# A new order of work in the opening of a decoder step: roots by tile, a scaled identity for the turn, half tiles first

## The chip, the cores and the metric

The kernel runs on one core of a Trainium2 chip. The metric is the device time of one execution in microseconds (us), where lower is better. Before the change it is 816.71 us, the median of three runs (815.47 to 817.28).

## The reference

One inference step of a hybrid decoder layer for 512 prompt tokens and 8 sample tokens of width 1024. The part around the change is the beginning: a root-mean-square norm, one wide input projection, and from its last eight columns the scalars beta and the decay of a gated delta rule.

```python
h = rms_norm(x, norm1_g)                    # x * rsqrt(mean(x*x) + 1e-6) * g, per token
z = einsum('btd,de->bte', h, w_in)          # 1024 -> 3336 columns
a_b, a_c, a_h, b_val, b_gate, qkv, c_gate, c_beta, c_alpha = split(z)
# A: gated short convolution; B: GLU, causal convolution of width 31, layer norm, swish
# C: convolution of width 4 and silu on q, k, v, then the delta rule with
beta = sigmoid(c_beta)
g = -exp(a_log) * softplus(c_alpha + dt_bias)
x = x + concat[A, B, C] @ w_out
x = x + hier_moe(rms_norm(x, norm2_g))      # 4 groups x 8 experts, top 2 in one group
```

A final norm follows. The convolution states and the delta state are outputs too.

## The kernel before

The program is written out by hand, one instruction stream for each engine, and semaphores join them. No scheduler moves anything: what stands first in an engine's function is issued first, and an instruction that waits holds up all behind it on its engine.

**Opening.** The 520 tokens stand as five tiles, four of 128 and one of 8, with tokens on the partitions. SyncE issues all loads (from L483): the tokens, the norm's weights `g1c`, all constants `cst` in one transfer, four weight tiles `wraw`, then parameters. A weight tile holds 1024 x 128 numbers, as 8 rows of 512 bytes on each partition; partition p takes rows 8p to 8p+7. ScalarE squares each token tile and sums it into `ss` (L612), then takes one root of all five sums (L617). VectorE takes the reciprocal (L1129), and for each tile writes the scaled tokens `hrow` (L1117). TensorE turns them with the identity, eight turns a tile (L1669). VectorE empties PSUM into `hT`, now with channels on the partitions, and multiplies by the norm's weights (L1124).

**Split for precision.** The projection works in two parts of each number: `hhi` and `whi` are rounded copies that ScalarE makes (L621, L625), `hlo` and `wlo` are what is left over, a subtraction on GpSimd or VectorE (L469, L959, L1180). GpSimd makes `hlo` of the first two token tiles and `wlo` of the first three weight tiles; VectorE makes the others.

**Projection.** There are 26 tiles of 128 output columns (L1695). Each has two halves, of 256 and of 264 tokens, and each half is 24 matmuls: 8 steps of channels times the three products hi by hi, lo by hi, hi by lo (L1708). Weights have four slots; the load of tile n waits for the projection of tile n-4 (L478). ScalarE empties a tile, takes the first tap of its convolution and rounds the weights of three tiles on (L731 to L748); VectorE does the other taps, gates, and the low parts of the weights (from L1265).

**Scalars.** After tile 1, `project_scalars` (L1684) computes the eight scalar columns in plain float32: for each of the five token tiles eight products with `hT` as the stationary side and `wba`, 8 columns wide, as the moving side (L1691). In iteration 3 the function `decays` on ScalarE (L631) and VectorE (L1159) turns them into gates and decays.

Behind the projection come the delta rule in two rounds of two heads, the output projection, routing, and the experts, whose weights stream from memory.

## Time and profile before

| | |
|---|---|
| Time, median of 3 | 816.71 us |
| The profiled execution, its own time | 815.65 us |
| Its span, first to last instruction | 813.8 us |
| TensorE busy | 667.7 us, 82% |
| VectorE busy | 365.6 us, 45% |
| ScalarE busy | 201.3 us, 25% |
| GpSimd busy | 137.8 us, 17% |
| Chain that ended last, by engine | TensorE 65%, transfers 15%, VectorE 13% |

The span is one execution under the hardware profiler, on whose time scale all rows below stand. A share of busy time is a mean over stages with different limits, so the stages have to be read one by one. The chain is followed back from the last instruction, at each step to what released it; it tells what the end waited for. The columns of a timeline are start, duration, engine, line, operation, and in brackets how long the engine sat idle before it and what released it. Neighbouring instructions of one kind stand as one row with a count. One float32 matmul that is no transpose stands as two records. In the windows of rows 1 the first four stretches show TensorE alone, the last one TensorE, its weight loads, VectorE, ScalarE and GpSimd.

### The profile page before, as it was taken

The numbers are of one execution on the slowest core, as the hardware profiler recorded it, in microseconds if no ns is written. First come the engines' busy times: TensorE is split into PE (matmuls) and PEld (weight loads), VectorE is DVE, ScalarE is ACT, GpSimd is POOL, SyncE is SP. The second block draws the span as 40 slices with busy tenths as digits, with TensorE's granted clock in tenths as the row PEclk, the third lists the DMA queues.
The fourth block names the chain that finished last, engine by engine and source line by source line (L and its number), as shares of the span: only waits on it lengthen the run. The fifth ranks groups of instructions, "written<-read, shape, count | busy, mean of one in ns | idle before, by whom it ended". The sixth has DMA issues, their size and how long they took to land.

```text
span 813.8 us, 12291 instructions
## 1 busy us (share of the span) xinstructions
PE 667.7 (82%) x4468; PEld 479.0 (59%) x4469; DVE 365.6 (45%) x621; ACT 201.3 (25%) x401; POOL 137.8 (17%) x211
## 2 busy tenths in 40 slices
PE   2699999999789999978999735988878899799740
PEld 2599998889788889964444411544434455354310
DVE  3743876879877577535213374111111111111128
ACT  5234365532232341242011100111111111111103
POOL 1700010211410010120000151121222212412110
PEclk9989999999979999997999855999999999899985
DMA  9012232223180000025600315399999999977925
GB/s 293 8 52 79 79 94 70 71 78 64 44 293 2 1 1 1 2 78 193 258 26 27 116 66 157 131 414 411 414 415 416 402 371 367 384 317 292 392 96 236
DMA packets 73209, 146.70 MB, mean 180 GB/s; under 512 B 14568, under 2 KB 50604, under 8 KB 64831
## 3 DMA queue, kind: packets, MB, share of 16 engines
q1 hardware_dynamic: 67327, 137.38, 45.8%
q0 software_dynamic: 5824, 8.54, 3.0%
q8 instruction: 37, 0.61, 0.3%
q14 instruction: 21, 0.17, 0.1%
HBM read 139.65 MB, written 16.60 MB: 192 GB/s over the span
## 4 chain that ended last, share of the span: by engine, by line
PE 65%; DMA 15%; DVE 13%; issue 3%; ACT 2%; SPq 1%; POOLq 0%; POOL 0%; DVEq 0%; ACTq 0%
PE ps L1708 19%; PE ps L1987 16%; DMA wd<-w_down 11%; PE ps L1782 8%; PE ps L1930 7%; PE ps L1913 2%; DMA xg<-h_rows,gcur 2%; DVE XX L1412 2%; PE ps L1951 1%; PE ps L2012 1%; DVE x L1638 1%; PE ps L1691 1%; PE ps L1731 1%; PE ps L1720 1%; DVE hrow L1117 1%
## 5 line engine op out<-in xcount | busy, mean ns | idle before, releaser
L1987 PE MATMUL ps<-gu,xT 128*64 128x256 f32 x1024 | 134.3, 407 | 27.4 <-DMA wd<-w_down 25.3
L1708 PE MATMUL ps<-hhi,whi 128*128 128x256 f32 (+1 forms) x416 | 121.1, 291 | 6.7 <-DVE hlo L469 5.1
L1987 PEld LDWEIGHTS ps<-gu,xT 128*64 128x64 f32 x1024 | 74.1, 145 | 83.8 <-issue 33.1
L1708 PE MATMUL ps<-hlo,whi 128*128 128x256 f32 (+1 forms) x416 | 119.1, 286 | 0.0
L1708 PE MATMUL ps<-hhi,wlo 128*128 128x256 f32 (+1 forms) x416 | 119.0, 286 | 0.0
L1708 PEld LDWEIGHTS ps<-hhi,whi 128*128 128x128 f32 x416 | 80.3, 193 | 12.4 <-POOL wlo L959 5.4
L1591 DVE SCALAR_TENSOR_TENSOR gact<-gth,ps 128x128 f32<-128x128 f32 x32 | 9.2, 288 | 164.2 <-ACT gth L922 164.2
L1708 PEld LDWEIGHTS ps<-hhi,wlo 128*128 128x128 f32 x416 | 80.4, 193 | 0.0
L1708 PEld LDWEIGHTS ps<-hlo,whi 128*128 128x128 f32 x416 | 80.1, 192 | 0.0
L1987 PE MATMUL ps<-wd,aT 128*64 128x512 f32 x256 | 62.9, 613 | 0.4 <-ACT aT L926 0.4
L1930 PE MATMUL ps<-wout,yT 128*128 128x512 f32 x128 | 59.2, 621 | 0.0
L1056 POOL DMA_INDIRECT expert_rows<-ysb,scur x32 | 32.4, 1012 | 147.4 <-DVE ysb L1622 142.9
L1622 DVE COPY ysb<-ps 128x512 f32<-128x512 f32 x32 | 22.1, 692 | 52.5 <-PE ps L1987 52.5
L1930 PEld LDWEIGHTS ps<-wout,yT 128*128 128x128 f32 x128 | 25.1, 199 | 30.6 <-issue 30.5
L1210 DVE SCALAR_TENSOR_TENSOR yT<-ub,parab,yT 128x512 f32<-128x512 f32 x60 | 41.9, 744 | 0.2
L1234 DVE SCALAR_TENSOR_TENSOR acc<-raw,parq,acc 128x544 f32<-128x544 f32 x36 | 28.5, 793 | 28.9 <-ACT acc L721 27.9
L926 ACT ACTIVATE aT<-ps 128x128 f32<-128x128 f32 x32 | 8.9, 278 | 130.7 <-PE ps L2047 130.7
L1412 DVE TENSOR_TENSOR XX<-XX,ps 128x1024 f32<-128x1024 f32 (+1 forms) x24 | 27.0, 1131 | 24.6 <-PE ps L1782 24.6
L1987 PEld LDWEIGHTS ps<-wd,aT 128*64 128x64 f32 x256 | 17.2, 139 | 24.5 <-issue 21.6
L1782 PE MATMUL ps<-XX,BT 128*128 128x128 f32 x192 | 26.1, 281 | 5.0 <-DVE XX L1412 5.0
L918 ACT ACTIVATE xT<-ps 128x1024 f32<-128x1024 f32 x16 | 16.4, 1024 | 49.8 <-PE ps L2069 33.5
L796 ACT ACTIVATE t<-ps 128x512 f32<-128x512 f32 x24 | 14.3, 597 | 57.9 <-PE ps L1782 57.9
(357 smaller groups left out, 1020.8 us busy)
## 6 DMA issues: line engine op xcount, KB each, us to landing
gu<-w_gate SPq DMA_DIRECT2D x32, 1024.0 KB, 9.1
gu<-w_up SPq DMA_DIRECT2D x32, 1024.0 KB, 11.3
wd<-w_down SPq DMA_DIRECT2D x32, 1024.0 KB, 14.8
wraw<-w_in SPq DMA_DIRECT2D x26, 512.0 KB, 4.1
wout<-w_out SPq DMA_DIRECT2D x1, 4096.0 KB, 16.3
yk<-expert_rows SPq DMA_DIRECT2D x8, 512.0 KB, 5.9
x<-x_prompt SPq DMA_DIRECT2D x4, 512.0 KB, 5.6
s<-state_delta SPq DMA_DIRECT2D x4, 512.0 KB, 6.1
```

The costliest lines, as they stand in the source:

```text
L796: copy(t1[z][:, :, :].rearrange("p a b -> p (a b)"), ps[:, B + 2, :], ACT.Copy).then_inc(T1_ready, 1)
L918: copy(xT[s][:, :, :], ps[:, 6:8, :].rearrange("p b (c t) -> p (b c) t", t=P), ACT.Copy).then_inc(xT_ready, 1)
L1056: nc.gpsimd.indirect_dma_start(out=yd, out_offset=bass.IndirectOffsetOnAxis(ap=scur[u][:, 0:1], axis=0), in_=ysb[u][:, :], in_offset=None, ...
L1210: ins = stt(out=y, in0=tap, scalar=parab[:, t, j:j + 1], in1=y, op0=ALU.mult, op1=ALU.add)
L1234: ins = stt(out=a[:, :], in0=r[:, j:j + CV], scalar=parq[:, QKV[m], j:j + 1], in1=a[:, :], op0=ALU.mult, op1=ALU.add)
L1412: tt(xx, xx, new, ALU.subtract).then_inc(X_ready, 1)
L1622: nc.vector.tensor_copy(ysb[u][:, :], ps[:, 4 + u % 2, :]).then_inc(y_ready, 1)
L1708: last = mm(ps[:, 2 * (n % 2) + half, 0:hi - lo], weights[:, c, :], h[:, c, lo:hi], start=c == 0 and j == 0, stop=c == KT - 1 and j == len ...
L1782: last = mm(ps[:, bank, i * P:(i + 1) * P], left(i), right(i), start=True, stop=True)
L1913: mm(ps[:, 4 + half, :], srow[:, 1, h * P:(h + 1) * P], vnd[half][:, :, :], start=True, stop=True).then_inc(s0_outer, 1)
L1930: last = mm(ps[:, 2 * (i % 2) + half, :], yT[:, k, tokens(ORDER[i])], wout[:, k, half * 512:(half + 1) * 512], start=k == 0, stop=k == KT - 1)
L1987: last = mm(ps[g * CAP:(g + 1) * CAP, bank, 0:width], left(c), right(c, g), start=c == 0, stop=c == steps - 1)
```

## The change

- **Loads.** The identity becomes a small transfer of its own, right behind the first tokens; then the norm's weights as 8 rows, the second tokens, the first weight tile, and the rest. Three weight tiles are issued ahead of the parameters, the fourth behind them. Partition p of a weight tile now takes the rows p, 128+p, 256+p and so on.
- **Roots by tile.** Each token tile has its square, its root and its reciprocal one behind the other. The first activation of ScalarE is a root of a constant.
- **Turn by a scaled identity.** VectorE multiplies the identity by the tile's factors (`diag`), and TensorE takes the product of the raw tokens and `diag`, a full float32 product in place of a transpose. `hrow` is gone. The norm's weights are turned by TensorE.
- **Low parts.** All on VectorE; GpSimd has none.
- **Half tiles first.** The first halves of weight tiles 0 and 1 are projected when the first two token tiles are ready, the turns of the last two token tiles between them, then the parameters' turns, then the second halves.
- **Scalars.** `wba`, widened to 32 columns with zeros, is the stationary side, `hT` the moving one, and the eight channel steps go to four column groups of TensorE, two steps to each. ScalarE copies the result (`zba`), and after the third tile five products with a constant (`C_PICK`) add the four groups and turn the scalars to tokens on partitions.
- GpSimd's semaphore `pool_passed` is merged into `cleared`.

On TensorE, the program's beginning, of the kernel before (`cst` is the table of constants with the identity, `ps` is PSUM, a trailing number tells buffers apart):

```order
L1669 MATMUL ps<-cst,hrow_118 128x128 x8
L1669 MATMUL ps<-cst,hrow_119 128x128 x8
L1669 MATMUL ps<-cst,hrow_118 128x128 x8
L1669 MATMUL ps<-cst,hrow_119 128x128 x8
L1669 MATMUL ps<-cst,hrow_118 128x8 x8
L1674 MATMUL ps<-cst,rowq 128x28 x12
L1677 MATMUL ps<-cst,rowab 128x52 x2
L1681 MATMUL ps<-cst,rowsb 128x120 x4
L1708 MATMUL ps<-hhi,whi_85 128x256
```

And the same place of the changed kernel; line numbers are those of the changed file, where L1697 is the turn of tokens and L1748 the projection:

```order
L1777 MATMUL ps<-cst,g1r 128x8
L1697 MATMUL ps<-diag_118,x 128x128 x8
L1697 MATMUL ps<-diag_119,x 128x128 x8
L1697 MATMUL ps<-diag_120,x 128x128 x8
L1748 MATMUL ps<-hhi,whi_85 128x256
...
L1697 MATMUL ps<-diag_121,x 128x128 x8
L1697 MATMUL ps<-diag_122,x 128x8 x8
L1748 MATMUL ps<-hhi,whi_86 128x256
...
L1706 MATMUL ps<-cst,rowq 128x28 x12
L1709 MATMUL ps<-cst,rowab 128x52 x2
L1713 MATMUL ps<-cst,rowsb 128x120 x4
```

Ahead of the first projected tile stood all turns; now three token tiles are turned, half a tile is projected, two token tiles are turned, and half of the next tile is projected before the parameters.

On VectorE, the program's beginning, of the kernel before:

```order
L1129 RECIPROCAL rstd<-ss 128x5
L1117 TENSOR_SCALAR hrow_118<-x,rstd 128x128x8
L1117 TENSOR_SCALAR hrow_119<-x,rstd 128x128x8
L1124 TENSOR_TENSOR hT<-ps,g1c 128x8x128
L1117 TENSOR_SCALAR hrow_118<-x,rstd 128x128x8
...
L1124 TENSOR_TENSOR hT<-ps,g1c 128x8x8
L469 TENSOR_TENSOR hlo<-hT,hhi 128x8x128 x2
L469 TENSOR_TENSOR hlo<-hT,hhi 128x8x8
```

And from the changed one, where L1139 scales the identity, L1152 is the low part of weights and L472 that of tokens:

```order
L1135 RECIPROCAL rstd<-ss 128x1
L1139 TENSOR_SCALAR diag_119<-cst,rstd 128x128
L1145 TENSOR_TENSOR hT<-ps,g1c 128x8x128
L1152 TENSOR_TENSOR wlo_111<-wraw_89,whi_85 128x1024
L1135 RECIPROCAL rstd<-ss 128x1
L1139 TENSOR_SCALAR diag_120<-cst,rstd 128x128
L1145 TENSOR_TENSOR hT<-ps,g1c 128x8x128
L472 TENSOR_TENSOR hlo<-hT,hhi 128x8x128 x2
L1145 TENSOR_TENSOR hT<-ps,g1c 128x8x128
```

The low parts of the first weights and of the first two token tiles now stand ahead of the emptying of the third token tile, and the scaled tokens are gone.

The diff, cut to its core; the order of the calls on VectorE is that of the rows above.

```diff
+    c[:, C_PICK:C_PICK + 8] = p[:, None] % 32 == np.arange(8)
...
-        hrow = [begin(f"hrow{s}", [P, KT, P]) for s in range(2)]
+        diag = [begin(f"diag{i}", [P, P]) for i in range(NT)]
+        g1r = begin("g1r", [KT, P])
...
-        wba = first("wba", [P, KT, 8])
+        wba = first("wba", [P, KT, 32])
+        zba = first("zba", [P, T])
...
-            w_in_cols = A["w_in"].rearrange("o (p c) e -> (o p) c e", c=KT)
+            w_in_cols = A["w_in"].rearrange("o (c p) e -> (o p) c e", p=P)
...
-            for i in range(TT):
+            def load_tokens(i):
                 sp.dma_start(x[:, i, :], xp[i]).then_inc(x_in[i], 16)
+
+            load_tokens(0)
+            sp.dma_start(cst[:, C_ID:C_ID + P], A["consts"][:, C_ID:C_ID + P]).then_inc(ident_in, 16)
+            sp.dma_start(g1r[:, :], A["norm1_g"].rearrange("o (c p) -> (o c) p", p=P)).then_inc(g1_in, 16)
+            load_tokens(1)
+            load_tile(0)
+            load_tokens(2)
+            load_tokens(3)
             sp.dma_start(x[0:NS, TT, :], A["x_sample"].rearrange("b o d -> (b o) d")).then_inc(x_in[TT], 16)
-            sp.dma_start(g1c[:, :], A["norm1_g"].rearrange("o (p c) -> (o p) c", c=KT)).then_inc(g1_in, 16)
-            sp.dma_start(cst[:, :], A["consts"]).then_inc(consts_in, 16)
-            for n in range(WSLOTS):
-                load_tile(n)
+            load_tile(1)
+            load_tile(2)
+            sp.dma_start(cst[:, C_ID + P:C_END], A["consts"][:, C_ID + P:C_END]).then_inc(consts_in, 16)
...
-            for i in range(NT):
+            act.wait_ge(cleared, 2)
+            copy(yT[:, 4, 0:1], epsc[:, :], ACT.Sqrt, bias=epsc[:, :])
+
+            def root_mean(i):
+                n = P if i < TT else NS
                 act.wait_ge(x_in[i], 16)
-                n = P if i < TT else NS
-                if i == 0:
-                    act.wait_ge(cleared, 1)
-                if i >= 2:
-                    act.wait_ge(x_squared, i - 1)
                 copy(yT[0:n, 2 * (i % 2):2 * (i % 2) + 2, 0:512], x[0:n, i, :].rearrange("p (a b) -> p a b", a=2), ACT.Square,
                      accum_out=ss[0:n, i:i + 1]).then_inc(x_squared, 1)
-
-            act.wait_ge(x_squared, NT)
-            act.wait_ge(cleared, 2)
-            copy(ss[:, :], ss[:, :], ACT.Sqrt, scale=1.0 / D, bias=epsc[:, :]).then_inc(x_squared, 1)
+                act.wait_ge(x_squared, 2 * i + 1)
+                copy(ss[0:n, i:i + 1], ss[0:n, i:i + 1], ACT.Sqrt, scale=1.0 / D, bias=epsc[0:n, :]).then_inc(x_squared, 1)
...
-            for i in range(NT):
-                round_tokens(i)
-                if i < WSLOTS - 1:
-                    round_weights(i)
+            root_mean(0)
+            root_mean(1)
+            round_weights(0)
+            root_mean(2)
+            round_tokens(0)
+            round_tokens(1)
+            root_mean(3)
+            root_mean(TT)
+            round_weights(1)
+            round_tokens(2)
+            round_tokens(3)
+            round_tokens(TT)
+            round_weights(2)
+
+            def gather_scalars():
+
+                act.wait_ge(ba_done, 1)
+                copy(zba[:, :].rearrange("p (a b) -> p a b", a=2), ps[:, 6:8, 0:HT], ACT.Copy).then_inc(ba_ready, 1)
...
-            for i in range(2):
-                rest_of_tokens(pool, i)
-
-            for n in range(WSLOTS - 1):
-                pool.wait_ge(w_hi, n + 1)
-                nc.gpsimd.tensor_tensor(wlo[n][:, :, :], wraw[n][:, :, :], whi[n][:, :, :], ALU.subtract).then_inc(w_lo, 1)
...
-            def scale_rows(i):
+            def scale_identity(i):
                 n = P if i < TT else NS
-                if i >= 2:
-                    vec.wait_ge(h_turned, i - 1)
-                nc.vector.tensor_scalar(hrow[i % 2][0:n].rearrange("t c p -> t p c"), x[0:n, i, :].rearrange("t (p c) -> t p c", c=KT),
-                                        rstd[0:n, i:i + 1], None, ALU.mult).then_inc(hrow_ready, 1)
+                vec.wait_ge(x_squared, 2 * i + 2)
+                nc.vector.reciprocal(rstd[0:n, i:i + 1], ss[0:n, i:i + 1]).then_inc(rstd_ready, 1)
+                vec.wait_ge(rstd_ready, i + 1)
+                if i == 0:
+                    vec.wait_ge(ident_in, 16)
+                nc.vector.tensor_scalar(diag[i][0:n, 0:n], ident[0:n, 0:n], rstd[0:n, i:i + 1], None, ALU.mult).then_inc(diag_ready, 1)
 
             def evacuate_h(i):
                 n = P if i < TT else NS
-                vec.wait_ge(h_turned, i + 1)
-                b = 2 * (i % 2)
+                vec.wait_ge(h_turned, i + 2)
+                b = 4 + 2 * (i % 2)
                 nc.vector.tensor_tensor(hT[:, :, tokens(i)], ps[:, b:b + 2, :].rearrange("p b (c t) -> p (b c) t", t=P)[:, :, 0:n],
                                         bcast(g1c[:, :], n), ALU.mult).then_inc(hT_ready, 1)
 
-            vec.wait_ge(g1_in, 16)
-            vec.wait_ge(x_squared, NT + 1)
-            nc.vector.reciprocal(rstd[:, :], ss[:, :]).then_inc(rstd_ready, 1)
-            vec.wait_ge(rstd_ready, 1)
-            for i in range(NT + 1):
-                if i < NT:
-                    scale_rows(i)
-                if i >= 1:
-                    evacuate_h(i - 1)
-            for i in range(2, NT):
-                rest_of_tokens(vec, i)
+            def rest_of_weights(n):
+
+                vec.wait_ge(w_hi, n + 1)
+                s = n % WSLOTS
+                nc.vector.tensor_tensor(wlo[s][:, :, :], wraw[s][:, :, :], whi[s][:, :, :], ALU.subtract).then_inc(w_lo, 1)
+
+            vec.wait_ge(h_turned, 1)
+            link(nc.vector.tensor_copy(g1c[:, :], ps[:, 3, 0:KT]))
...
...
-            pe.wait_ge(consts_in, 16)
-
-            for i in range(NT):
+            def turn_tokens(i):
                 n = P if i < TT else NS
-                pe.wait_ge(hrow_ready, i + 1)
+                pe.wait_ge(diag_ready, i + 1)
+                pe.wait_ge(x_in[i], 16)
                 if i >= 2:
                     pe.wait_ge(hT_ready, i - 1)
+                b = 4 + 2 * (i % 2)
                 for c in range(KT):
-                    last = turn(ps[:, 2 * (i % 2) + c // 4, c % 4 * P:c % 4 * P + n], hrow[i % 2][0:n, c, :], ident[0:n, 0:n])
+                    last = mm(ps[:, b + c // 4, c % 4 * P:c % 4 * P + n], x[0:n, i, c * P:(c + 1) * P], diag[i][0:n, 0:n],
+                              start=True, stop=True)
                 last.then_inc(h_turned, 1)
...
+            def turn_parameters():
+
+                pe.wait_ge(rows_in, 8 * 16)
+                pe.wait_ge(hT_ready, NT)
...
             def project_scalars():
 
                 pe.wait_ge(small_in, 4 * 16)
-                pe.wait_ge(hT_ready, NT)
+                pe.wait_ge(params_ready, 3)
+                for half in range(2):
+                    for c in range(0, KT, 4):
+                        for g in range(4):
+                            last = mm(ps[32 * g:32 * g + 32, 6 + half, 0:HT], wba[:, c + g, :], hT[:, c + g, half * HT:(half + 1) * HT],
+                                      start=c == 0, stop=c == KT - 4)
+                last.then_inc(ba_done, 1)
+
+            def gather_scalars():
+
+                pe.wait_ge(ba_ready, 1)
                 for i in range(NT):
                     n = P if i < TT else NS
-                    for c in range(KT):
-                        last = mm(ps[0:n, 7, i * 8:(i + 1) * 8], hT[:, c, tokens(i)], wba[:, c, :], start=c == 0, stop=c == KT - 1)
+                    last = mm(ps[0:n, 7, i * 8:(i + 1) * 8], zba[:, tokens(i)], cst[:, C_PICK:C_PICK + 8], start=True, stop=True)
                 last.then_inc(ba_done, 1)
 
 
-            def project(n):
+            def project(n, half):
                 s = n % WSLOTS
                 pe.wait_ge(w_lo, n + 1)
-                if n == 0:
-                    pe.wait_ge(hT_ready, NT)
-                if n >= 2:
+                if n < 2:
+                    pe.wait_ge(h_lo, NT if half else 2)
+                elif half == 0:
                     pe.wait_ge(z_evac, n - 1)
-                for half, (lo, hi) in enumerate(((0, 256), (256, T))):
-                    if n == 0:
-                        pe.wait_ge(h_lo, NT)
-                    parts = [(weights[s], h) for weights, h in ((whi, hhi), (wlo, hhi), (whi, hlo))]
-                    for c in range(KT):
-                        for j, (weights, h) in enumerate(parts):
-                            last = mm(ps[:, 2 * (n % 2) + half, 0:hi - lo], weights[:, c, :], h[:, c, lo:hi],
-                                      start=c == 0 and j == 0, stop=c == KT - 1 and j == len(parts) - 1)
-                last.then_inc(z_done, 1)
+                lo, hi = ((0, 256), (256, T))[half]
+                parts = [(weights[s], h) for weights, h in ((whi, hhi), (wlo, hhi), (whi, hlo))]
+                for c in range(KT):
+                    for j, (weights, h) in enumerate(parts):
+                        last = mm(ps[:, 2 * (n % 2) + half, 0:hi - lo], weights[:, c, :], h[:, c, lo:hi],
+                                  start=c == 0 and j == 0, stop=c == KT - 1 and j == len(parts) - 1)
+                if half:
+                    last.then_inc(z_done, 1)
 
...
+            pe.wait_ge(ident_in, 16)
+            pe.wait_ge(g1_in, 16)
+            turn(ps[:, 3, 0:KT], g1r[:, :], ident[0:KT, 0:KT]).then_inc(h_turned, 1)
+            for i in range(3):
+                turn_tokens(i)
+            project(0, 0)
+            turn_tokens(3)
+            turn_tokens(TT)
+            project(1, 0)
+            pe.wait_ge(consts_in, 16)
+            turn_parameters()
+            project(0, 1)
+            project(1, 1)
+            project_scalars()
             for n in range(NZ + 4):
-                if n < NZ:
-                    project(n)
-                if n == SCALARS:
-                    project_scalars()
+                if 2 <= n < NZ:
+                    project(n, 0)
+                    project(n, 1)
+                if n == SCALARS + 1:
+                    gather_scalars()
```

## Rows read from the trace of the kernel before

**Rows 1.** Windows: stretch, us, busy (count) by engine, granted clock, DMA share, GB/s
```profile
19.30:29.90 10.60, 7.64 (x42) 1.00 0.23 36
35.00:40.60 5.60, 5.60 (x26) 1.00 0.01 3
...
54.70:58.30 3.60, 3.60 (x31) 0.50 0.02 5
58.40:61.80 3.40, 3.40 (x18) 0.58 0.00 0
...
90.00:219.00 129.00, 128.91 (x981) 117.57 (x980) 104.72 (x141) 55.08 (x101) 23.90 (x42) 1.00 0.27 68
```

**Rows 2.** Chain of waits, opening: start us, us, what held it
```profile
2.21 7.03 DMA x<-x_prompt
...
11.47 1.28 ACT L617
...
14.88 1.96 PE ps L1669 x8
...
29.14 5.65 DVE hlo L469 x2
```

**Rows 3.** Chain of waits, first tiles of the projection
```profile
34.92 14.36 PE ps L1708 x96
49.28 9.12 PE ps L1691 x80
58.39 13.02 PE ps L1708 x96
...
78.69 11.75 PE ps L1708 x96
```

**Rows 4.** Timeline of ScalarE, in the opening and in the output stage
```profile
4.82 1.06 ACT L612 ACTIVATE yT<-x 128x1024 f32<-128x1024 f32 x1 [2.54 <-DMA x<-x_prompt]
...
19.09 1.04 ACT L625 ACTIVATE whi<-wraw 128x1024 fp32r<-128x1024 f32 x1
...
419.95 1.06 ACT L846 ACTIVATE sqj<-x 128x1024 bf16<-128x1024 f32 x1 [11.95 <-DVE x L1462]
...
421.13 0.29 ACT L848 ACTIVATE ss<-ss,epsc 128x1 f32<-128x1 f32 x1
```

**Rows 5.** Timeline of VectorE in the opening and behind the first tile
```profile
16.86 1.23 DVE L1124 TENSOR_TENSOR hT<-ps,g1c 128x1024 f32<-128x1024 f32 x1 [0.97 <-PE ps L1669]
...
27.31 7.46 DVE L469 TENSOR_TENSOR hlo<-hT,hhi 128x1024 fp32r<-128x1024 f32 x3
...
36.41 0.17 DVE L1148 TENSOR_SCALAR lnh<-parab 128x4 f32<-128x4 f32 x1
...
49.18 1.22 DVE L1180 TENSOR_TENSOR wlo<-wraw,whi 128x1024 fp32r<-128x1024 f32 x1
```

**Rows 6.** Timeline of TensorE: turns of parameters, float32 products, samples' output projection
```profile
26.99 1.46 PE L1674 MATMUL ps<-cst,rowq 28*128 28x28 f32 x12
...
227.93 1.91 PE L1782 MATMUL ps<-cst,brep 128*128 128x128 f32 x8
...
233.42 1.06 PE L1782 MATMUL ps<-cv,cv 128*128 128x128 f32 x8
...
377.66 5.83 PE L1922 MATMUL ps<-wout,yT 128*8 128x256 f32 x64
```

**Rows 7.** Transfers: all in 3 to 16 us; projection's weights, issue to landing
```profile
DMA packets 3492, 4.57 MB, mean 352 GB/s; under 512 B 264, under 2 KB 2917, under 8 KB 3364
...
DMA to landing us min/median/max: 4.0/4.1/11.6
```

**Rows 8.** Timelines of ScalarE and VectorE, first convolution
```profile
43.82 0.60 ACT L681 ACTIVATE raw<-ps 128x512 f32<-128x512 f32 x1
...
44.53 0.75 ACT L721 ACTIVATE acc<-raw,parq 128x544 f32<-128x544 f32 x1
...
45.38 2.43 DVE L1234 SCALAR_TENSOR_TENSOR acc<-raw,parq,acc 128x544 f32<-128x544 f32 x3 [8.62 <-ACT acc L721]
```

87 lines of the change are left out of this document (51 added, 36 removed).

## The prediction

> **What bounds the kernel now.** I read the whole span first, as the chain of waits, and then only its opening, because nothing else is edited. The reader is to see three stretches in it. From 0 to 34.9 us the chain is a relay with no TensorE work worth the name: the last of four token loads, five squares, a table load, one root over all five tiles, then VectorE scaling, TensorE turning, VectorE emptying, and at the end VectorE making the low parts of the tokens until 34.8 [rows 2]. From 34.92 TensorE carries the chain almost alone: two projected tiles, 9.12 us of scalars' projection, two more tiles that take 13.02, a wait of some 1.5 us for a low part of the weights, and from 78.69 on tiles back to back [rows 3]. In 90 to 219 us TensorE is busy 128.9 of 129 us, while VectorE has 24 us free and ScalarE 74 [rows 1]: there the stage is bound by TensorE, so a start that is earlier by some us ends earlier by as much, and what comes later (the delta rule, routing, experts) waits for signals and not for a clock on the wall. What I have to find is therefore one number: when the fourth tile's projection ends. Before, that is 71.41 (58.39 plus 13.02).
>
> One view more matters, the windows of TensorE. At 35.0 to 40.6 it is never idle and yet starts 26 matmuls in 5.6 us, 0.213 us each: 256 columns in that time is 1.2 GHz, though the row says 1.00 granted. Later the same matmul takes 0.122 (11.75 us for 96), the 2.4 GHz level. It falls again in the scalars' stretch, granted 0.50, and is still there in most of 58.4 to 61.8, where 18 tile matmuls start [rows 1, 3].
>
> **What the rows give as prices.**
> - A root for one tile: square 1.06, root 0.29. The output stage has just this order, from 419.95 to 421.42, with room for no table load between them; I take 1.5 us per tile [rows 4].
> - Rounding a tile of tokens or weights: 1.04 on ScalarE [rows 4]. Emptying a turned tile: 1.23 on VectorE. A low part on VectorE: 1.22 alone, but three of them, the last of 8 tokens only, took 7.46 while GpSimd worked beside them [rows 5]. GpSimd now has none of this work, so I take 1.2, and 0.2 for the 8 tokens.
> - A product of 128x128x128 in float32 shows as two records. Eight records last 1.91 us at the low level and 1.06 at the high one, each with some 0.2 in which the last one drains beside the next [rows 6]. A tile of eight products is then 3.4 or 1.8 us; its turn before was 1.96 [rows 2].
> - Scaling the identity: not in the trace. Below it a 4-column operation of 0.17, above it the 1.2 us of a 1024-column one [rows 5]; 128 columns are near the small one, so 0.2, and 0.45 with the reciprocal. Both ends move the sum by under 1 us, since this step is waited for on the chain twice at most.
> - Half of a projected tile: 24 matmuls, 2.9 us high, 5.1 low [rows 1, 3].
>
> **The opening, worked out.** Loads: the bytes flow at 352 GB/s in 3 to 16 us [rows 7]. The first tokens are used at 4.82 before [rows 4], and nothing stands ahead of them now either. The first weight tile is fourth in line, 1.6 MB after the start: at that rate 4.6 us of flow from about 2.5, and 512-byte pieces are slower, so 8.3. A lone tile lands in 4.1 us and the slowest took 11.6 from issue [rows 7]; it is now issued near 2.7, so the bounds are 6.8 and 14.3. The value lies nearer the lone tile because only 1.1 MB stand ahead of it.
>
> ScalarE: root 0 at 4.8 to 6.3, root 1 to 7.8, weights 0 rounded 8.3 to 9.4, third tokens landed at about 9.8, root 2 to 11.3. TensorE: tile 0 turned 6.8 to 10.2 at the low level. VectorE: tile 0 emptied to 11.5, low weights 0 to 12.7, diagonal 2 to 13.1. Tile 1 turned to 13.5, emptied to 14.7, rounded to 15.8 (ScalarE), its low part done at 17.0, tile 0's before it. Tile 2 is turned beside this. So the first half of tile 0's projection starts at 17.1, where the whole of it started at 34.92. I let it run at the high level: TensorE then has been fed with full products since 6.8, with one gap of about 2 us.
>
> From there TensorE and VectorE alternate. First half of tile 0: to 20.0. Roots 3 and 4 on ScalarE end at 18.7, weights 1 rounded 19.7, low part 20.9. Tokens 3 turned 20.0 to 21.8, the eight samples to 22.4, first half of tile 1 to 25.3. Meanwhile VectorE: emptied 3 to 23.0, low part 2 to 24.3, samples emptied 24.5, low part 3 to 25.7, samples' 25.9. The parameters' eighteen turns come after the samples are emptied; twelve of them took 1.46 us at the low level [rows 6], so I take 2.2 for all, 25.3 to 27.5. Then the second half of tile 0 to 30.4, of tile 1 to 33.3.
>
> Scalars: 80 records of 8 columns, 9.12 us, become 16 products of 32 rows by 260 columns in four column groups, 32 records. The samples' output projection has the same form: 64 records of 256 columns in 5.83 us [rows 6]. Half of that, 2.9 us, is the upper bound for 32; if that stretch ran at the low level, the high one gives 1.4 or 1.5. I take 1.6, to 34.9. The third tile: 5.9, to 40.8. Now a new wait. The gathering products need the copy of the scalars on ScalarE, and ScalarE reaches it only after the second convolution's tanh. Counted from the end of tile 0: copies and first tap 1.7, convolution 2.4 beside rounding and the table load, tanh 0.7, copies of tile 1 and first tap 1.7, convolution 2.4 behind one low part, tanh 0.7, copy 0.7, some 10.8 in all with the hand-overs [rows 4, 8]. That is 41.2, so TensorE waits 0.4. Behind it stand tile 3 and all later ones. Gathering: 10 records of the old form at 9.12/80 = 0.11 us [rows 3], 1.1, to 42.3. Fourth tile to 48.2.
>
> **The sum.** 71.41 - 48.2 = 23.2 us. Of this, 13.0 is gained up to the end of tile 0's projection (about 43.4 before, 34.92 plus 8.5; now 30.4), and 10.2 behind it, mostly the scalars (9.12 for 1.6 plus 1.1 plus 0.4) and the low-clock part of the third tile that follows them (13.02 against two times 5.9); tile 1's first half, done ahead, gives the rest. The wait for low weights after the fourth tile [rows 3] hangs on the decays, which keep their place on ScalarE and VectorE, so I leave it as it is. The profiled execution took 815.65 us, 1.85 around its span of 813.8; 815.65 - 23.2 = 792.5. The median of the runs is 1.06 higher, 816.71, and from it the forecast is **793.5 us**.
>
> Costs put at nothing. The weights' other row order keeps 1024 pieces of 512 bytes; a load has nearly three tiles, some 17 us, to land, and needs 4.1 [rows 7]. The second part of the constants, the parameters and the scalars' weights come later in the queue than before, but are wanted at 25 us and beyond; by bytes they have landed near 20. If they came at 28, each us more would be one us lost. The increments on GpSimd's other semaphore and its first arithmetic operation, now in the delta rule, lie beside idle time of that engine.
>
> The trace shows turns from 19.3 to 29.9, busy for 7.6 of 10.6 us, after which TensorE starts at the low level all the same [rows 1]. The Trainium skill (TensorE: Matmul & The Clock Gate, Part 4: PE-mode transpose) states that transposes do not count as busy for the clock gate. By that rule the new products, which are no transposes, raise the clock in the opening as I assume; by a reading that only the pauses held it down, the rival below would hold. The table load ahead of the root stands as 1.28 us, from 11.47, and VectorE has the tokens turned by TensorE from 14.88 on, with root, scaling and hand-overs between [rows 2]. The same skill (ScalarE: Activation LUTs, What ACT_TABLE_LOAD costs) adds a drain of 1.38 us to every switch. By the row one load less gives 1.3 here, by the page 2.7; the measured one stands in my times.
>
> **The rivals.**
> - *The clock stays low in the opening.* For it: the low level lasted 5.6 us of dense work from 34.92 [rows 1], and the opening has a gap before 17.1. Then the first half takes 5.1 instead of 2.9. The clock rises in what follows, as 17.1 plus 5.6 is 22.7; tokens 3 take 2.3, not 1.8, and all later steps shift by some 2.5, tile 0 ending at 32.7. Gain 20.9 or less the gather's wait, which moves along: 795.8. If it stayed low until 30, two halves and turns cost 5 in all: 798.5.
> - *The loads come late.* First weights at 14.3, the upper bound: the rounding ends 15.4, root 2 at 16.9, tokens 0 and 1 rounded 18.0 and 19.1, so the first half starts near 20.5, 3.4 late. 797. Against it: only 1.1 MB stand ahead.
> - *Slower than before: weights in the new row order land too slowly.* Each partition now reads eight rows that lie 128 rows apart. Four slots hide latency but not rate: a tile is consumed every 5.9 to 6.9 us. From 6.3 us a load the stage is bound by loads; to eat 23.2 us over the 22 tiles left it has to be 7.4. At 8.5 us it is 22 times 2.2, 48 less 23: 841. Against it: piece size and count are unchanged, 4.1 us to land, and the DMA share is 0.27 in the stage [rows 1, 7].
> - *It does not do what it says:* VectorE becomes the bound of the opening by more than I count (it has some 15 us of work between 6 and 26), for example if low parts stay at 2.5 us. Eight of them before the second halves, six on the path, cost 1.3 each: 8 us, 801.
>
> **How the numbers follow.** The forecast with its own scatter, 791 to 795: 0.62. Clock low: 0.20. Loads late: 0.08. VectorE slow: 0.05. A better opening than worked out, with turns high from the start or the gather's wait gone, 789 to 791: 0.03. Slower: 0.02. The range 790 to 798.5 leaves out the last and parts of others, about 1 in 8. The measurement tells 0.2%, 1.6 us, from no change; every case but the slow one lies below that, so faster 0.97, same 0.01, slower 0.02.
>
> **What would show it.** In the new profile: the first tile matmul near 17 and not 35; no table load between square and root in the opening; the turning products with 0.21 us a record at first and 0.11 by tile 2; low parts at 1.2 on VectorE; 32 records of scalars in 1.4 to 2.9 us and no granted 0.50 behind them; the gather waiting for ScalarE's copy by under 1 us; the fourth tile ending near 48, and everything from there as before, 23 us earlier. A first tile matmul after 21, or a stage from the fourth tile on that is not as long as before, would make the prediction wrong.

## The result, and the profile after

The changed kernel takes 795.33 us (median of four runs, 792.93 to 800.38), the kernel before 816.09 in the same comparison. The ratio is 0.9747, 95% interval 0.9706 to 0.9787. A second series of six runs gave 0.9743 (0.9713 to 0.9774). Forecast was 793.5, range 790 to 798.5. The profiled execution took 792.93 with a span of 791.0, against 815.65 and 813.8: 22.8 us of span are gone, where the working had 23.2.

The chain of waits of the changed kernel, opening and first tiles. In its file L1697 is the turn of tokens, L1748 the projection, L1724 the scalars, L1733 the gather, L1152 and L472 the low parts:

```profile
6.41 3.79 PE ps L1697 x16
...
16.61 3.08 PE ps L1748 x24
19.68 3.66 PE ps L1697 x32
23.35 3.03 PE ps L1748 x24
...
28.05 5.84 PE ps L1748 x48
33.89 1.89 PE ps L1724 x32
35.78 5.94 PE ps L1748 x48
41.72 0.92 PE ps L1733 x10
42.65 5.96 PE ps L1748 x48
...
54.69 1.15 DVE wlo L1152
...
55.88 11.76 PE ps L1748 x96
```

It answers to [rows 2, 3]. The first tile matmul starts at 16.61 and not at 34.92. The two tiles are now four halves of about 3 us, 19.68 to 23.35 being turns between two of them. The scalars are 1.89 plus 0.92 where they were 9.12, and the fourth tile ends at 42.65 plus 5.96, 48.61, where it was 71.41. That is 22.8 us, all that the span lost: from there to the end both executions take 742.4 us. The wait for the sixth tile's low part (54.69) is still there.

Windows of TensorE of the changed kernel (stretch, us, busy, clock, DMA share, GB/s):

```profile
15.20:16.60 1.40, 0.00 (x0) 1.00 0.97 404
16.60:19.60 3.00, 2.99 (x25) 1.00 0.92 202
...
33.90:35.80 1.90, 1.90 (x33) 1.00 0.45 94
35.80:41.70 5.90, 5.90 (x50) 1.00 0.23 68
```

There is a pause of 1.4 us and then 25 matmuls in 3.0 us, the high level at once; before, the same matmuls ran at the low one after a pause [rows 1]. The column of the granted clock reads 1.00 in the opening of both kernels, so the level there has to be read from the time per matmul, 0.12 us at the high one and 0.21 at the low one. Behind the scalars the clock stays at 1.00, where [rows 1] had 0.50 and 0.58.

Timeline of ScalarE of the changed kernel:

```profile
4.29 1.06 ACT L622 ACTIVATE yT<-x 128x1024 f32<-128x1024 f32 x1 [1.88 <-DMA x<-x_prompt]
...
5.47 0.29 ACT L625 ACTIVATE ss<-ss,epsc 128x1 f32<-128x1 f32 x1
7.96 1.06 ACT L622 ACTIVATE yT<-x 128x1024 f32<-128x1024 f32 x1 [2.20 <-DMA x<-x_prompt]
...
9.44 1.06 ACT L633 ACTIVATE whi<-wraw 128x1024 fp32r<-128x1024 f32 x1
...
40.78 0.59 ACT L652 ACTIVATE zba<-ps 128x520 f32<-128x520 f32 x1
```

Square and root follow each other without a table load. The second tokens are squared at 7.96 after 2.20 us without work; I had them at 6.3. The copy for the gather ends at 41.37, before the third tile does (41.72).

Timeline of VectorE of the changed kernel, to be read beside [rows 5]:

```profile
6.07 0.29 DVE L1139 TENSOR_SCALAR diag<-cst,rstd 128x128 f32<-128x128 f32 x1
...
10.23 1.23 DVE L1145 TENSOR_TENSOR hT<-ps,g1c 128x1024 f32<-128x1024 f32 x1 [0.27 <-PE ps L1697]
11.37 1.22 DVE L1152 TENSOR_TENSOR wlo<-wraw,whi 128x1024 fp32r<-128x1024 f32 x1
...
14.03 2.43 DVE L472 TENSOR_TENSOR hlo<-hT,hhi 128x1024 fp32r<-128x1024 f32 x2
```

A diagonal takes 0.29, and a low part 1.22: two take 2.43, where three took 7.46 with GpSimd at work. One row of TensorE tells when the clock rose; it is the turn of the third token tile:

```profile
13.03 2.05 PE L1697 MATMUL ps<-diag,x 128*128 128x128 f32 x16 [0.36 <-DVE diag L1139]
```

The first tile's 16 records held the chain for 3.79 us, the low level; these 16 take 2.05, the high one.

### The profile page after: what moved, and what is told of

The parts are those of the page before. It is cut to its first block, busy times and chain, and to the rows that moved or that the text cites. A ratio compares the mean times of both kernels' runs of the same rounds, so it can differ in the third digit from the quotient of the medians.

```text
span 791.0 us, 12310 instructions
## 1 busy us (share of the span) xinstructions
PE 660.4 (83%) x4471; PEld 471.0 (60%) x4472; DVE 360.3 (46%) x631; ACT 201.7 (26%) x406; POOL 124.4 (16%) x207
## 4 chain that ended last, share of the span: by engine, by line
PE 65%; DMA 16%; DVE 12%; issue 3%; ACT 2%; SPq 1%; POOLq 0%; POOL 0%; DVEq 0%; ACTq 0%
PE ps L1748 19%; PE ps L2043 15%; DMA wd<-w_down 12%; PE ps L1838 8%; PE ps L1986 7%; PE ps L1969 2%; DMA xg<-h_rows,gcur 2%; DVE XX L1440 2%; PE ps L2007 1%; DVE x L1666 1%; PE ps L2068 1%; PE ps L1772 1%; PE ps L1761 1%; PE ps L1697 1%; DMA expert_rows<-yo,osid 1%
## 5 line engine op out<-in xcount | busy, mean ns | idle before, releaser
L1748 PE MATMUL ps<-hhi,whi 128*128 128x256 f32 (+1 forms) x416 | 119.5, 287 | 3.1 <-DVE wlo L1152 1.6
L1748 PE MATMUL ps<-hlo,whi 128*128 128x256 f32 (+1 forms) x416 | 117.3, 282 | 0.0
L1748 PE MATMUL ps<-hhi,wlo 128*128 128x256 f32 (+1 forms) x416 | 117.2, 282 | 0.0
L1748 PEld LDWEIGHTS ps<-hhi,whi 128*128 128x128 f32 x416 | 78.3, 188 | 9.1 <-issue 6.2
L1748 PEld LDWEIGHTS ps<-hhi,wlo 128*128 128x128 f32 x416 | 78.4, 189 | 0.0
L1748 PEld LDWEIGHTS ps<-hlo,whi 128*128 128x128 f32 x416 | 78.2, 188 | 0.0
L1650 DVE COPY ysb<-ps 128x512 f32<-128x512 f32 x32 | 22.1, 691 | 52.9 <-PE ps L2043 52.9
L1152 DVE TENSOR_TENSOR wlo<-wraw,whi 128x1024 fp32r<-128x1024 f32 x26 | 31.5, 1215 | 1.7 <-ACT whi L633 1.6
L2043 PEld LDWEIGHTS ps<-wd,aT 128*64 128x64 f32 x256 | 17.2, 139 | 24.5 <-issue 21.6
```

The source lines that it names most:

```text
L1152: nc.vector.tensor_tensor(wlo[s][:, :, :], wraw[s][:, :, :], whi[s][:, :, :], ALU.subtract).then_inc(w_lo, 1)
L1650: nc.vector.tensor_copy(ysb[u][:, :], ps[:, 4 + u % 2, :]).then_inc(y_ready, 1)
L1748: last = mm(ps[:, 2 * (n % 2) + half, 0:hi - lo], weights[:, c, :], h[:, c, lo:hi], start=c == 0 and j == 0, stop=c == KT - 1 and j == len ...
L2043: last = mm(ps[g * CAP:(g + 1) * CAP, bank, 0:width], left(c), right(c, g), start=c == 0, stop=c == steps - 1)
```

## The experiments

All experiments but the one on the kernel before start from the changed kernel. Besides the time I read where the fourth tile ends, as behind it nothing differs unless said. Times are medians; ratios are to the kernel before with 95% intervals.

**1. The changed kernel again (no edit), twice.**

> The changed kernel once more, to separate what moves from execution to execution from what the change moved. Theory: the opening is the same each time (first tile matmul 16.6, fourth tile ended 48.6, both within 0.5 us), and the spread of the runs (792.9 to 800.4) lies behind the projection, in stages that the change does not touch; then the ratio to before is 0.972 to 0.977. Rival: the spread is made in the opening, by the order in which the tokens and the first weights land or by the clock level there; then the fourth tile's end in this profile differs from 48.6 by some of it, up to 4 us.

Measured: 795.35 us, ratio 0.9743 (0.9713 to 0.9774). First half tile at 16.66, fourth tile ended at 48.64, both within 0.05 of the first profile. The span was 792.7: 744.1 us behind the fourth tile instead of 742.4.

> The changed kernel, one more look. Two of four profiles that share its opening showed TensorE granted 0.6 to 0.7 at 23.3 to 28 us, costing 1.5 us, and two did not. Theory: it is a matter of the execution and not of the edits, since those lie behind it; this look shows either, and the stages behind the projection differ by up to 3 us from the last look. Rival: the edits caused it; then it is absent here for a third time.

Measured: 793.36 us in one run; first half tile 16.61, fourth tile ended 48.61, no dip of the clock. Over all ten profiles that share the code behind the fourth tile (both kernels and experiments 1 to 7), that part took 741.4 to 747.0 us: the spread is made there, in the delta rule's stage and in the experts, and the opening of the unedited changed kernel was the same to 0.05 us in its three profiles. The dip of the clock (seen in experiments 3 and 8) is absent in all three of these, as the rival expected. That does not prove the rival, since the edits of those experiments act behind the dip in time; what causes it stays open.

**2. The scalars alone, put into the kernel before.**

```diff
-                    for c in range(KT):
-                        last = mm(ps[0:n, 7, i * 8:(i + 1) * 8], hT[:, c, tokens(i)], wba[:, c, :], ...)
+                for half in range(2):
+                    for c in range(0, KT, 4):
+                        for g in range(4):
+                            last = mm(ps[32 * g:32 * g + 32, 6 + half, 0:HT], wba[:, c + g, :], hT[:, c + g, ...], ...)
...
+                if n == SCALARS + 1:
+                    gather_scalars()
```

> The kernel before with the scalars' projection in four column groups alone. Theory: 9.12 us become 1.9 plus 0.9 for the gather, and the granted 0.50 behind it is gone, worth 1.3 more in the third tile: the fourth tile ends at 71.4 minus 7.6, near 63.8, time 8 us under before, ratio 0.990. Rival: the third tile ran low for another reason; then 6.3 us, ratio 0.992, with the granted clock still falling. Other rival: with the 9 us gone the gather waits for ScalarE, whose chain of two convolutions stands closer behind; then 1 to 2 us less gain.

Measured: 809.64 us, ratio 0.9906 (0.9870 to 0.9941). Its chain, same columns, L1704 the scalars, L1713 the gather:

```profile
34.26 13.45 PE ps L1730 x96
47.71 1.89 PE ps L1704 x32
49.60 5.93 PE ps L1730 x48
...
56.45 5.95 PE ps L1730 x48
```

From the start of the scalars to the end of the fourth tile 14.7 us pass, 22.1 before: 7.4, where 7.6 were expected. The rest of the 9.0 us by which this tile ends earlier (62.40) lies ahead of the edit: the start was 0.7 earlier in this execution and the clock rose sooner in the first tiles. The third tile took 5.93, at the high level: the low clock did come from the narrow products. The median is 7.7 us under before and the profiled execution only 4.4, because the part behind the fourth tile was the longest of all here, 747.0.

**3. The old scalars in the changed kernel.** The reverse edit: 40 narrow products, 80 records, `wba[:, c, 0:8]` as the moving side, no gather.

> The changed kernel with the scalars' projection of before (80 narrow products, no gather). The same three answers from the other side. Theory: 6.3 us for the instructions and 1.3 for the low clock behind them, 7.6 us slower than the changed kernel, fourth tile ended at 56.2, granted clock 0.50 behind the scalars. Rival: 6.3 alone.

Measured: 806.30 us, ratio 0.9864 (0.9825 to 0.9902), 11 us over the changed kernel; the fourth tile ends at 60.78, 12.2 later and not 7.6. Chain and windows of this execution (L1722 the scalars, L1737 the projection):

```profile
23.44 4.51 PE ps L1737 x24
...
35.47 11.37 PE ps L1722 x80
46.84 13.94 PE ps L1737 x96
```

```profile
35.40:38.00 2.60, 2.60 (x26) 1.00 0.64 153
38.00:41.00 3.00, 3.00 (x17) 0.53 0.27 80
...
46.80:50.00 3.20, 3.20 (x17) 0.50 0.00 0
```

The clock falls some 2.7 us into the scalars, and not 5.2 as before the change, so that they take 11.37 and not 9.12. The low level lasts longer into the next tiles: 13.94, where the kernel before had 13.02 and the high level would give 11.9. Another 1.5 lies in the half tile at 23.44, where the clock had fallen too; that is ahead of the edit. The mechanism was right and its price larger than expected. Why the clock fell sooner here is not shown.

**4. Turns without the product.**

```diff
-                    last = mm(ps[:, b + c // 4, c % 4 * P:c % 4 * P + n], x[0:n, i, c * P:(c + 1) * P], diag[i][0:n, 0:n],
-                              start=True, stop=True)
+                    last = turn(ps[:, b + c // 4, c % 4 * P:c % 4 * P + n], x[0:n, i, c * P:(c + 1) * P], ident[0:n, 0:n])
```

The product with the factors is gone, so this kernel leaves out the norm's factors; its waits are those of the changed kernel.

> The changed kernel with transposes of the raw tokens by the plain identity in place of the products with the scaled one; the waits stay, the factors of the norm are left out of the result (they are near 1). Theory: transposes do not raise the clock, so the first half tile starts at the low level, 24 matmuls in 5.1 us or until the clock rises, not 3.08; the turns themselves are shorter at the start (1.97 for 3.4) but the chain up to the first half tile is held by VectorE, so it starts near 15.5 to 16.6. The fourth tile then ends 2 to 3 us later than 48.6. Rival: pauses alone set the level; then turns as dense as these raise it too, the first half tile takes 3.1, and with turns of half the records the fourth tile ends 1 to 2 us earlier, near 47.

Measured: 794.47 us, ratio 0.9722 (0.9687 to 0.9756), the same as the changed kernel. TensorE's timeline and the chain of this execution (L1697 turns, L1747 projection):

```profile
6.39 1.97 PE L1697 MATMUL ps<-cst,x 128*128 128x128 f32 x8 [1.54 <-DVE diag L1139]
9.24 1.97 PE L1697 MATMUL ps<-cst,x 128*128 128x128 f32 x8 [0.88 <-DVE diag L1139]
12.23 1.97 PE L1697 MATMUL ps<-cst,x 128*128 128x128 f32 x8 [1.02 <-DVE diag L1139]
15.80 0.55 PE L1747 MATMUL ps<-hhi,whi 128*128 128x256 f32 x1 [1.60 <-DVE hlo L472]
```

```profile
15.80 5.40 PE ps L1747 x24
21.20 1.46 PE ps L1697 x16
22.66 3.03 PE ps L1747 x24
```

The half tile at 15.80 takes 5.40 us, the low level, where it took 3.08 behind products. So the part on the clock held: turns of 1.97 us with pauses of about 1 between them left it low, while 48 records of products left it high (the third turn, 2.05 us). The sum did not. The fourth tile ends at 47.90, 0.7 earlier than in the changed kernel: 0.8 from the earlier start, 2.2 from half as many records in the turns at 21.2 (1.46 against 3.66), less 2.3 for the low clock. Here the turns were also less dense, so density and kind of instruction are not told apart by this run.

**5. Low parts of the first tiles on GpSimd.** Two tokens' and three weights' low parts go back, in the order weights 0, tokens 0, tokens 1, weights 1, weights 2.

> The changed kernel with the low parts of the first two token tiles and first three weight tiles on GpSimd, as before. Theory: GpSimd takes 2.8 for tokens and 3.3 for weights where VectorE takes 1.2, and slows VectorE beside it (two 1.22 become up to 2.6); the low part of the second token tile ends at 19.4, the first half tile starts there and not at 16.6, and the fourth tile ends 3 to 5 us later than 48.6. Rival: VectorE, freed of five operations, runs ahead and makes up for it; then it ends within 1 us of 48.6.

Measured: 795.41 us, ratio 0.9753 (0.9721 to 0.9785), the same. GpSimd's timeline:

```profile
10.05 2.36 POOL L982 TENSOR_TENSOR wlo<-wraw,whi 128x1024 fp32r<-128x1024 f32 x1 [7.99 <-ACT whi L633]
12.62 4.67 POOL L472 TENSOR_TENSOR hlo<-hT,hhi 128x1024 fp32r<-128x1024 f32 x2 [0.21 <-ACT hhi L629]
18.48 2.38 POOL L982 TENSOR_TENSOR wlo<-wraw,whi 128x1024 fp32r<-128x1024 f32 x1 [1.18 <-ACT whi L633]
```

A low part takes 2.36 on GpSimd, not the 2.8 and 3.3 that I had from the kernel before. That is not because VectorE is idle here: it emptied PSUM beside the first two rows and had nothing to do beside the third, and the times are alike. In the kernel before it scaled tokens and made low parts beside GpSimd, and both were slow. Scaling beside GpSimd is slow here too: a diagonal, 0.29 us alone, took 0.67 and 1.06, while emptying stayed at 1.23:

```profile
16.32 1.06 DVE L1149 TENSOR_SCALAR diag<-cst,rstd 128x128 f32<-128x128 f32 x1
```

The first half tile starts at 17.44, behind a pause of 2.84 us and at the high level all the same (3.06 us), and the fourth tile ends at 49.44, 0.8 later. That is the rival's outcome (within 1 us), and the theory's 3 to 5 us failed by a factor of four or more. In this execution the second tokens were squared at 7.08, 0.9 before those of the changed kernel, and the third at 10.12, 0.7 before, so with the same loads the price might be up to 1 us more, still under the theory's.

**6. All turns first, then whole tiles.**

```diff
             for i in range(3):
                 turn_tokens(i)
-            project(0, 0)
             turn_tokens(3)
             turn_tokens(TT)
-            project(1, 0)
             pe.wait_ge(consts_in, 16)
             turn_parameters()
-            project(0, 1)
-            project(1, 1)
+            pe.wait_ge(h_lo, NT)
+            for n in range(2):
+                project(n, 0)
+                project(n, 1)
```

> The changed kernel with all turns first and then whole tiles. Theory: the first tile starts when the last low part of the tokens is done, near 24, after the parameters' turns, and four halves of 2.95 follow: scalars begin near 36.5 and not 33.9, fourth tile ends 2.5 to 3.5 us later. Rival: the pause of TensorE between turns and tiles puts it back to the low level, as before the change; then 2.5 us on top, 5 to 6 in all. Other rival: half tiles first are worth nothing, since TensorE's work is the same and VectorE ends as early; then within 0.5.

Measured: 799.28 us, ratio 0.9785 (0.9754 to 0.9816); the fourth tile ends at 56.20, 7.6 later. Windows and chain:

```profile
15.20:16.60 1.40, 0.00 (x0) 1.00 1.04 434
16.60:19.60 3.00, 1.54 (x10) 0.86 0.97 178
19.60:21.50 1.90, 1.90 (x10) 0.50 0.47 46
...
28.00:33.80 5.80, 5.80 (x34) 0.62 0.00 0
```

```profile
18.06 6.69 PE ps L1697 x32
...
27.96 13.54 PE ps L1748 x96
```

TensorE has nothing from 15.07 to 18.06; the clock reads 1.00 for another 0.7 us of turns and 0.50 behind that. Turns of the last two token tiles take 6.69 for 3.66, the parameters' turns 2.8 for 1.7, the two tiles 13.54 for 11.95. So 5.8 of the 7.6 us are the clock and 1.8 the order itself. The rival with the pause named the right mechanism, and its 5 to 6 us were too small for this profile. The medians differ by 4.0 us only: the part behind the fourth tile was the shortest of all here, 741.4, and whether every execution loses the full 7.6 can't be told from one profile.

**7. All roots before the first diagonal.** ScalarE does five squares and roots first, VectorE waits for the last.

> The changed kernel with all squares and roots first and the scaled identities only after the last. Theory: the last root ends near 15.3 (fourth tokens land near 12, then two squares), the first turn starts there and not at 6.4, the first half tile near 25, and TensorE has turned all tiles by then; fourth tile ends 6 to 8 us later than 48.6. Rival: the roots are hidden because VectorE's chain is the bound; then under 3 us.

Measured: 802.85 us, ratio 0.9822 (0.9789 to 0.9855). The first turn starts at 15.52, the first half tile at 25.73, and the fourth tile ends at 57.73, 9.1 later (7.5 by the medians): all of the 9.1 us between the first turns (6.41 and 15.52) comes through. I had expected two of them back, from turns done ahead; the order of the calls doesn't allow that.

**8. What is left, taken out.** First only the low part of the sixth weight tile ahead of the decays.

```diff
                 if n == SCALARS + 2:
+                    rest_of_weights(n + 2)
                     decays()
```

> The changed kernel, and in iteration 3 VectorE makes the low part of the sixth weight tile ahead of the decays, while it is idle, and not behind them. Theory: the wait of TensorE between the fifth and the sixth tile (54.5 to 55.88) goes, everything behind is 1.4 us earlier, ratio to the changed kernel 0.998. Rival: the wait is taken over by the next low part, since VectorE has a convolution and two gates to catch up there; then 0 to 0.5 us.

Measured: 794.69 us, ratio 0.9729 (0.9699 to 0.9759). From the third tile's gather on, four tiles run without a pause, 23.14 us for 192 matmuls where 24.98 passed: 1.8 us gained. But the half tile at 23.42 took 4.56 us with a granted clock of 0.62 in 23.3 to 26.4 (it fell at 24.1), as in experiment 3, and gave 1.5 back. Then the samples' turn as well:

```diff
-                nc.vector.tensor_scalar(diag[i][0:n, 0:n], ident[0:n, 0:n], rstd[0:n, i:i + 1], None, ALU.mult)...
+                dst, src = (diag[i][:, :], ident) if i < TT else (hs[:, :], x[0:NS, TT, :])
+                nc.vector.tensor_scalar(dst, src, rstd[0:n, i:i + 1], None, ALU.mult)...
...
+                    if i == TT:
+                        last = turn(out, hs[:, c * P:(c + 1) * P], ident[0:n, 0:n])
```

> The changed kernel with two edits: the low part of the sixth weight tile ahead of the decays, and the eight samples scaled as rows on VectorE and turned by eight transposes, where they took 16 narrow float32 records. Theory: the narrow records of the samples cost 1.8 us, of which 0.9 goes, and they are what lets the granted clock fall near 23.4 in some executions (as 80 narrow records of the scalars do), so the dip is gone as well; the sixth tile no longer waits, 1.4. The tile behind the scalar sums (two narrow records, at 67.63 in the changed kernel) starts at 65.3, time 2.3 us under the changed kernel, more where that had the dip. Rival: the dip comes from the pause at 15.1 to 16.6 and not from the narrow records; then it shows here in some profiles as well. Other rival: VectorE needs about 1 us for the samples' rows on its chain and gives the 0.9 back: 66.2.

Measured: 790.51 us, ratio 0.9682 (0.9657 to 0.9707), the lowest median here. Its interval is clear of the second series of the changed kernel (0.9713 to 0.9774) and touches that of the first (0.9706 to 0.9787) at its edge. Its chain:

```profile
19.62 1.78 PE ps L1704 x16
21.41 0.59 PE ps L1702 x8
...
26.70 5.84 PE ps L1754 x48
...
41.30 23.14 PE ps L1754 x192
```

The samples' turn takes 0.59, so both turns are 2.37 for 3.66. The scalar sums come at 64.44, 3.2 us before those of the changed kernel at 67.63. VectorE takes 0.74 for the samples' rows, in time for an operation that waited for ScalarE anyway. The dip is absent here, which one profile doesn't prove. The profile's span, 784.7, is 6.3 shorter; the other 3.1 lie in the output projection, where TensorE was granted 0.98 for 0.95, and in the experts. I have no cause for these.

**9. The opening pulled forward.** On top of 8: five products of zeros before the first turn, the second tokens loaded ahead of the identity, the first half tile ahead of the third tile's turn.

> The same, and the opening pulled forward: five products of zeros on TensorE from about 1.5 us to raise the clock ahead of the first turn, the second tokens loaded ahead of the identity, the first half tile ahead of the third token tile's turn, and ScalarE and VectorE orders to match. Theory: the first turn takes 1.8 and not 3.4 us, the second tokens land at 6.5 and not at 7.96, the first half tile starts at 14.7 and not at 16.6, and all is 1.9 us earlier still, scalar sums near 63.4. Rival: the identity lands later behind the second tokens and takes the place of the root, and the zeros do not last to the first turn, so the clock is low again; then the first half tile starts at 16 or later and the gain is under 0.6.

Measured: 795.12 us, ratio 0.9740 (0.9715 to 0.9765), slower than experiment 8's second kernel and level with the changed one. TensorE's timeline and chain:

```profile
1.47 4.38 PE L1785 MATMUL ps<-wba 128*128 128x256 f32 x10 [1.47 <-POOL wba L976]
...
7.30 3.84 PE L1705 MATMUL ps<-diag,x 128*128 128x128 f32 x32 [0.78 <-DVE diag L1142]
15.43 0.36 PE L1755 MATMUL ps<-hhi,whi 128*128 128x256 f32 x1 [4.29 <-DVE hlo L473]
```

```profile
15.43 4.60 PE ps L1755 x24
```

The zeros did their work: 32 records of turns take 3.84 us, the high level. The half tile starts at 15.43, 1.1 us earlier, not 1.9: the identity, now behind the second tokens, came only at 6.3, and on ScalarE the third tokens' square and root (11.61 to 13.07) stand between the roundings of the first and the second tokens. TensorE is idle for 4.29 us ahead of the half tile, since the first turns are over sooner and the third one no longer stands there. The clock falls at 15.7, the half tile takes 4.60, and the sums come at 66.64, 2.2 later than in experiment 8's second kernel. That adds up as 1.1 gained at the start, 1.5 lost in the half tile by the clock, and 1.8 lost because the third tile's turn now stands behind the half tile. The rival had the late identity but put the low clock in the wrong place, and neither had the moved turn, the largest of the three. The median is 4.6 later. Behind the sums this profile has 723.3 us, as the changed kernel's has (723.4), where that of experiment 8 had 720.3; since its edits are in this kernel too, those 3 us are not shown to be their work.

## Why the prediction was right, and where its terms were off

**The bound.** It said that one number decides, the end of the fourth tile, and that the stage behind it is as long as before. In the first pair of profiles that holds to 0.1 us (742.4 both). Its value, 48.2, was 0.4 from the measured 48.6, and that is partly luck: the terms below were off by up to 1.3 us each and cancelled.

**The first half tile** at 17.1 came at 16.61. Two steps inside were off and cancelled or hid. The second tokens landed 1.6 us later than the byte rate said, but tile 0's turn at the low clock lasted to 10.2 in any case. The weights were rounded at 9.44 and not 8.3, for the same reason: ScalarE had its second root to do first. VectorE's low parts at 1.2, the diagonal at 0.3 to 0.45 with its reciprocal, the turn at 3.4 (3.79 with its last record) stood as predicted. So did the table load: one less in the relay, and in both kernels the next activation starts 0.01 us behind the 1.28 us of the load.

**The clock** was the assumption with the largest rival, 0.20, and it held in the profile: high from the third turn at 13.03 on, and through the pause up to 16.61. The median alone would not tell the two apart, since 795.33 lies nearer to the rival's 795.8 than to 793.5. The experiments show how near it was. With a pause of 2.99 us instead of 1.4 it fell (experiment 6), with one of 2.84 it did not (experiment 5), behind transposes it was low (experiment 4), and in two executions it fell at 24.1 and 24.5, some 1 us behind the samples' narrow records, and cost 1.5 us. The executions without a profile may or may not have had this dip.

**The mis-sized term** is the turn of the samples. "The eight samples to 22.4" gave them 0.6 us; with the turn of tokens 3 they took 3.66 and not 2.4. A float32 record with 8 moving columns costs as much as one with 128, about 0.11 us, when its stationary side has 128 columns; I had priced it by its moving columns. The kernel before shows which side counts. Its 80 records of scalars all had 8 moving columns: 47 of those with 128 stationary columns took 5.0 us at the high level, and the last 16, the samples' with 8 stationary columns, only some 0.6 us at the low one. The parameters' turns took 1.67 for 2.2 and gave 0.5 of it back, the start of the first half tile another 0.5.

**The scalars:** 1.89 for 1.6, gather 0.92 for 1.1, and the wait for ScalarE's copy, 0.4 in the working, was zero with 0.35 to spare. This wait at nothing made up for the 0.3 of the scalars. Experiment 2 measured the part by itself, 7.4 us behind the first two tiles; the working had 6.0 for the instructions and some 1.2 for the clock.

**The gain by parts**, each undone alone, as the later end of the fourth tile: roots by tile 9.1, scalars 12.2 (1.5 of it a dip ahead of the edit), half tiles 7.6, low parts on VectorE 0.8. They sum to more than 22.8; several contain the clock. By the medians the same four are 7.5, 11.0, 4.0 and 0.1. That VectorE takes all low parts was the smallest; in the working it stood behind most steps. The product in place of a transpose was worth nothing by itself (experiment 4, 0.7 us the other way). Three parts were not undone: scaling the identity and not the tokens, the order of the loads, and the rows of the weights.

**The median** came 1.8 us above its forecast, while the profiled execution, 792.93, came 0.4 above the 792.5 worked out for it. The likely rest is the spread behind the projection, 741.4 to 747.0 us over ten profiles, which the first three runs of before did not show in full; the profiled execution was the fastest of its four. The runs without a profile can't show where their time went.

The rivals: loads did not come late (a weight tile lands in 3.8 us, 4.1 before [rows 7], so the new row order did not slow the loads), VectorE was not the bound beyond what was counted, and nothing was slower.

## What to carry to other kernels

Follow one number, the moment at which the dense engine has done a fixed piece of work, through the whole relay ahead of it; if the stage behind is bound by that engine, the difference is the gain. Price narrow float32 products by record and by the columns of their stationary side, not by the moving ones, and count what they do to the clock of what follows. A pause ahead of dense work can have a price beyond its length, so pulling a part forward is worth something only if the work behind it comes forward too.

## What the runs showed of the hardware that was not expected

- GpSimd makes a low part of 128x1024 in 2.36 us with VectorE idle or emptying PSUM (experiment 5), and took about 2.8 to 3.3 while VectorE scaled tokens and made low parts (the kernel before); VectorE took 1.22 alone and about 2.5 beside it. An identity scaled by VectorE took 0.29 alone and 0.67 and 1.06 beside GpSimd (experiment 5), while emptying PSUM stayed at 1.23.
- TensorE kept its high level over a pause of 1.4 to 1.5 us behind the third turn in every profile that had it, and over 2.84 in experiment 5, and lost it over 2.99 and 4.29 (experiments 6 and 9), there only 0.7 and 0.3 us after work had begun again. The two cases of 2.84 and 2.99 are one profile each, and what follows the pause differs too, so that the length alone decides is not shown. In two of the profiles it fell to 0.50 granted, at 24.1 and 24.5 us, with TensorE never idle since 16.7, some 1 us behind 16 records of 8 columns; in the others with the same records it did not.
- The scalars' 32 records of 260 columns in four column groups took 1.89 us in each profile that had them, 0.06 us a record, where a full-width record of 128 columns took 0.11.
